# The first group of an FFN as a split group, fed in smaller jobs, with ring pieces between them

## The reference

```python
    x = x + rms_norm(y, norm_mix_post[l])          # y: the mixer's w_out product
    h = rms_norm(x, norm_ffn_pre[l])
    f = conv_gated_mlp(h, w_up[l], conv_ffn_w[l], conv_ffn_bias[l], w_down[l])
    x = x + rms_norm(f, norm_ffn_post[l])

def conv_gated_mlp(h, w_up, conv_w, conv_b, w_down):
    up = h @ w_up                                  # 2048 -> 2 * 5632
    up = causal_depthwise_conv(up, conv_w) + conv_b    # 3 taps over the tokens
    gate, val = jnp.split(up, 2, axis=-1)
    return (jax.nn.silu(gate) * val) @ w_down
```

## Time and profile before

| | us |
|---|---|
| median of 3 runs (lowest, highest) | 2581.59 (2580.73, 2586.28) |
| the profiled execution | 2575.56 |
| its span | 2573.8 |
| TensorE busy | 2519.6 (98%) |
| VectorE busy | 1678.2 (65%) |
| ScalarE busy | 1140.7 (44%) |
| weight loads and weight reads, moved | 547.89 MB, 213 GB/s |

### The profile page before, as it was taken

The page is one execution under the profiler, slowest core; times in us unless marked ns, Lnnn a source line. Parts: engine busy times, 40 slices in busy tenths (PEclk is TensorE's granted clock), DMA queues, the critical chain, the costliest instruction groups (busy, mean ns, idle before and its releaser), DMA issues.

```text
span 2573.8 us, 42624 instructions
## 1 busy us (share of the span) xinstructions
PE 2519.6 (98%) x18920; PEld 2367.0 (92%) x18920; DVE 1678.2 (65%) x2034; ACT 1140.7 (44%) x1311; POOL 11.2 (0%) x24
## 2 busy tenths in 40 slices
PE   6999999999999999999999999999899999999998
PEld 2688799999998999999999999899899889988997
DVE  5366666677787755555555579877677556764775
ACT  3422555544445434434434553054455445443554
POOL 0000000000000000000000000000000000000000
PEclk9999999999999999999999999999999999999999
DMA  9976665577885755555555555455355555555543
GB/s 399 372 245 231 217 223 199 207 293 293 304 290 201 288 194 184 193 192 186 196 184 193 182 179 188 153 184 177 151 180 197 196 194 184 195 185 192 191 172 129
DMA packets 77223, 547.89 MB, mean 213 GB/s; under 512 B 8848, under 2 KB 8976, under 8 KB 12272
## 3 DMA queue, kind: packets, MB, share of 16 engines
q1 hardware_dynamic: 74304, 533.53, 57.8%
q0 software_dynamic: 2448, 11.14, 1.2%
q10 hardware_dynamic: 288, 0.50, 0.1%
HBM read 539.90 MB, written 5.24 MB: 212 GB/s over the span
## 4 chain that ended last, share of the span: by engine, by line
PE 94%; DVE 3%; DMA 2%; ACT 1%; issue 1%; SPq 0%; DVEq 0%; ACTq 0%
PE acc L295 23%; PE acc L299 23%; PE acc L297 22%; PE acc L315 5%; PE acc L316 5%; PE acc L317 5%; PE acc L352 3%; DMA raw<-in_w_mod 1%; PE mp L382 1%; PE mp L315 1%; PE mp L317 1%; PE mp L316 1%; DVE macc L426 1%; DVE wlo L263 1%; PE mp L441 0%
## 5 line engine op out<-in xcount | busy, mean ns | idle before, releaser
L263 DVE TENSOR_TENSOR wlo<-raw,whi 128x1024 fp32r<-128x1024 f32 x779 | 942.1, 1223 | 660.2 <-ACT whi L254 658.5
L254 ACT ACTIVATE whi<-raw 128x1024 fp32r<-128x1024 f32 x779 | 817.8, 1058 | 1164.4 <-PE acc L299 860.1
L295 PE MATMUL acc<-hh,whi 128*128 128x256 f32 x3360 | 938.9, 279 | 7.7 <-issue 5.5
L299 PE MATMUL acc<-hl,whi 128*128 128x256 f32 x3360 | 941.3, 280 | 0.0
L297 PE MATMUL acc<-hh,wlo 128*128 128x256 f32 x3360 | 934.3, 278 | 0.0
L295 PEld LDWEIGHTS acc<-hh,whi 128*128 128x128 f32 x3360 | 635.6, 189 | 12.9 <-issue 11.3
L299 PEld LDWEIGHTS acc<-hl,whi 128*128 128x128 f32 x3360 | 631.9, 188 | 0.0
L297 PEld LDWEIGHTS acc<-hh,wlo 128*128 128x128 f32 x3360 | 630.1, 188 | 0.5
L299 PE MATMUL acc<-ml,whi 128*128 128x256 f32 x1536 | 430.1, 280 | 0.0
L295 PE MATMUL acc<-mh,whi 128*128 128x256 f32 x1536 | 426.6, 278 | 0.1
L297 PE MATMUL acc<-mh,wlo 128*128 128x256 f32 x1536 | 426.5, 278 | 0.0
(11 more groups left out here) (341 smaller groups left out, 2197.8 us busy)
## 6 DMA issues: line engine op xcount, KB each, us to landing
raw<-in_w_in SPq DMA_DIRECT2D x98, 1024.0 KB, 4.9
raw<-in_w_mod SPq DMA_DIRECT2D x96, 1024.0 KB, 5.8
raw<-in_w_up SPq DMA_DIRECT2D x88, 1024.0 KB, 4.9
raw<-in_w_mlp_in SPq DMA_DIRECT2D x64, 1024.0 KB, 4.9
raw<-in_w_mlp_out SPq DMA_DIRECT2D x64, 1024.0 KB, 4.9
raw<-in_w_down SPq DMA_DIRECT2D x44, 1024.0 KB, 4.9
raw<-in_w_out SPq DMA_DIRECT2D x32, 1024.0 KB, 5.1
raw<-in_w_fourier_out SPq DMA_DIRECT2D x8, 1024.0 KB, 6.1
```

The lines of the kernel that those rows point to most:

```text
L254: nc.scalar.activation(ring(whi, xh, st.p), raw_slot(k)[:, 2 * GC * j:2 * GC * (j + 1)], ACT.Copy)\
L263: nc.vector.tensor_tensor(ring(wlo, xl, st.p), raw_slot(k)[:, 2 * GC * j:2 * GC * (j + 1)], ring(whi, xh, st.p).bitcast(f32), ALU.subtract ...
L295: nc.tensor.matmul(dst, whi[:, r, cols], hi[:, kt, :], start=begin, stop=False, skip_group_check=True)
L299: last = nc.tensor.matmul(dst, whi[:, r, cols], lo[:, kt, :], start=False, stop=kt == nkt - 1, skip_group_check=True)
```

## The change

The four plain slots of the FFN's first group become four ordinary slots, so that group is split like the others, and the order of the loads becomes the ordinary one. Its x comes in nine jobs: two of one tile and seven of two. ScalarE writes `hh` directly from x with the gain; `hf` is not made. VectorE makes `hl` per tile (one instruction: x times gain minus `hh`) one job behind x, with a ring piece behind some jobs (`FFN_BEHIND`, plus one behind the third). Three more pieces stand around the two folds. `feature_piece` has a hook `tile`, which waits for each tile's job. `zz_sums` moves from before the last slot of the first group to before the fourth piece of the second. In `ffn_pair` the exceptions for the first group go. Cut to its core:

```diff
-STREAM += "d" * (MLP_CHUNKS * 32 - 16 + 12 + 2) + "ffff" * 3 + "d" * (2 + 6 + 16 + 2) + "ffff"
-STREAM += "d" * (2 + 20 * 4 + 44)
+STREAM += "d" * (MLP_CHUNKS * 32 - 16 + 12 + 2) + "ffff" * 3 + "d" * (2 + 6 + 16)
+STREAM += "d" * (2 * 4 + 20 * 4 + 44)
...
-        N2_JOBS = [(0, 1), (1, 1), (2, 2), (4, 4), (8, 4), (12, 4)]
+        N2_JOBS = [(0, 1), (1, 1)] + [(a, 2) for a in range(2, KT, 2)]
+        FFN_BEHIND = (0, 0, 0, 1, 1, 1, 1, 0, 0)
...
-                    last = nc.scalar.activation(hf[:, kt, :], xT2[:, kt, :], ACT.Copy,
+                    last = nc.scalar.activation(hh[:, kt, :], xT2[:, kt, :], ACT.Copy,
                                                 scale=pcol("norm_ffn_pre_2", kt))
-                last.then_inc(S["hf_ok"], 1)
-                act.wait_ge(S["hf_ok"], i + 1)
-                nc.scalar.activation(hh[:, a:a + n, :], hf[:, a:a + n, :], ACT.Copy).then_inc(S["fh_ok"], 1)
+                last.then_inc(S["fh_ok"], 1)
+                C(st, FFN_BEHIND[i], met=0)
+            C(st, 3, met=0)
...
+            next_x(0)
+            for i, (a, n) in enumerate(N2_JOBS):
+                if i + 1 < len(N2_JOBS):
+                    next_x(i + 1)
+                dve.wait_ge(S["xm_ok"], i + 1)
+                dve.wait_ge(S["fh_ok"], i + 1)
+                for kt in range(a, a + n):
+                    last = nc.vector.scalar_tensor_tensor(hl[:, kt, :], xT2[:, kt, :], pcol("norm_ffn_pre_2", kt),
+                                                          hh[:, kt, :].bitcast(f32), ALU.mult, ALU.subtract)
+                last.then_inc(S["fl_ok"], 1)
+                if i == 2:
+                    C(1, met=0)
+                C(FFN_BEHIND[i], met=0)
+            C(1, met=0)
             fold(xy, um1, False, "xy_ok")
+            C(1, met=0)
             dve.wait_ge(S["gy_sq"], 4)
             dve.wait_ge(S["yy_ok"], 3)
             fold(yy, um2, False, "yy_ok")
-            for i, (a, n) in enumerate(N2_JOBS):
-                dve.wait_ge(S["fh_ok"], i + 1)
-                nc.vector.tensor_tensor(hl[:, a:a + n, :], hf[:, a:a + n, :], hh[:, a:a + n, :].bitcast(f32),
-                                        ALU.subtract).then_inc(S["fl_ok"], 1)
             C(1, met=0)
             dve.wait_ge(S["zz_ps"], 1)
...
-            def zz_sums(s):
-                if s == 3:
+            def zz_sums(k0):
+                if k0 == 6:
...
-                        if c + p + v:
-                            mm_feature(pe, st, v, hh, hl, 1, ready=split if c + p == 0 else None)
+                        first = c + p == 0
+                        mm_feature(pe, st, v, hh, hl, 1, each=zz_sums if first and v else None,
+                                   tile=next_ready if first and not v else None)
```

More of the change, by code:

```diff
@@ L283, in group_done, with feature_piece @@
             eng.wait_ge(S["used"], st.e)
-        def feature_piece(pe, st, i, hi, lo, k0, nkt=KT, w=GC):
+        def feature_piece(pe, st, i, hi, lo, k0, nkt=KT, w=GC, tile=None):
             r = st.p % 4
@@ L290, in feature_piece @@
                 kt = k0 + k
+                if tile:
+                    tile(kt)
                 for t in range(w // P):
@@ L326, in acc_wait, with mm_feature @@
             st.f[i] += evictions
-        def mm_feature(pe, st, i, hi, lo, frees, nkt=KT, w=GC, ready=None, free=None, each=None):
+        def mm_feature(pe, st, i, hi, lo, frees, nkt=KT, w=GC, ready=None, free=None, each=None, tile=None):
             if free:
@@ L339, in mm_feature @@
                     each(k0)
-                feature_piece(pe, st, i, hi, lo, k0, nkt, w)
+                feature_piece(pe, st, i, hi, lo, k0, nkt, w, tile)
         def plain_group(pe, st, i, h, frees, each, between, n):
@@ L1003, in ffn_pair @@
                 for v in range(2):
[L1004 to L1010, removed]
+                    st.e += 8
+                    group_done(act, st)
+                    hi_piece(act, st)
                     act.wait_ge(acc_free[v], F_OUT2[v] + n + 2 * c + 1)
@@ L1019, in ffn_pair @@
                     last.then_inc(S["ct_ok"], 1)
-                    if n + v:
-                        hi_piece(act, st)
+                    hi_piece(act, st)
                     act.wait_ge(S["cd_ok"], 2 * n + v + 1)
@@ L1640, in _, with next_x @@
             own(nc.vector.reciprocal(rstd[:, 0, :], root[:, :]))
-            for i, (a, n) in enumerate(N2_JOBS):
+            def next_x(i):
+                a, n = N2_JOBS[i]
                 if a == 12:
@@ L1669, in ffn_pair @@
                 for v in range(2):
-                    if n < v:
-                        C(7, met=8)
-                    elif n:
-                        st.e += 8
-                    if n + v:
-                        group_done(dve, st)
-                    else:
-                        dve.wait_ge(S["f_used"], 16)
+                    st.e += 8
+                    group_done(dve, st)
                     up, um = ((up1, um1), (up2, um2))[v]
@@ L1695, in ffn_pair @@
                     last.then_inc(S["cd_ok"], 1)
-                    if n + v:
-                        lo_piece(dve, st)
+                    lo_piece(dve, st)
                     if v == 0:
@@ L1710, in ffn_pair @@
                             .then_inc(S["fid_ok"], 1)
-                    if n + v:
-                        C(4 if n + v == 11 else 6, met=0)
+                    C(4 if n + v == 11 else 6, met=0)
             def down_add(c, g):
@@ L2028, in _, with next_ready @@
                 last.then_inc(S["yq_ps"], 1)
-            def hf_each(kt):
-                for i, (a, n) in enumerate(N2_JOBS):
-                    if kt == a:
-                        pe.wait_ge(S["hf_ok"], i + 1)
-            def zz_sums(s):
-                if s == 3:
+            def next_ready(kt):
+                pe.wait_ge(S["fl_ok"], jobs_upto(kt + 1, N2_JOBS))
+            def zz_sums(k0):
+                if k0 == 6:
                     for k, total, sem in ((0, xy, "xy_ok"), (1, yy, "yy_ok")):
@@ L2042, in zz_sums @@
                     last.then_inc(S["zz_ps"], 1)
-            plain_group(pe, st, 0, hf, 1, hf_each, zz_sums, 3)
-            def split(s):
-                pe.wait_ge(S["fl_ok"], jobs_upto(4 * s + 4, N2_JOBS))
             def ffn(st, c, pairs, slots):
```

14 lines of the change are left out of this document (3 added, 11 removed).

## The result

| | before | changed |
|---|---|---|
| median, us | 2580.11 (10 runs, 2573.72 to 2586.28) | 2588.80 (10 runs, 2582.66 to 2590.94) |
| ratio, 95% interval | | 1.0036 (1.0027 to 1.0045) |
| the profiled execution, us (its span) | 2575.56 (2573.8) | 2588.48 (2586.6) |

The change makes the kernel slower by 0.36%, 9.3 us of 2580 (7.0 to 11.6). The forecast was 2588.7 and slower by 7.1 us; it stood on a median of 2581.59 from three runs of the kernel before, and ten give 2580.11. A second timing of the same kernel on another occasion gave 1.0024 (1.0015 to 1.0034). From here on "the stretch" runs from the end of the w_out_2 product (the start of the second norm's sums less TensorE's 0.69 us of idle time, 1809.39 in the trace before, 1812.50 after) to the start of the second FFN group's eviction.

A forecast was written before the change was run, and what follows sets the result against it. TensorE was taken to bound the kernel (98% busy). Terms -4.7 + 2.0 + 6.7 + 2.9 + 0.2 gave +7.1 us: 2588.7 us for the runs, 2582.7 for a profiled execution; range 2582.5 to 2595.

The forecast's parts named there:

- The plain group's 27.9 us against 22.1 and the first group's end: First FFN group: split matmuls replace slower plain fp32 ones, VectorE sets the pace, group ends 4.7 us earlier.
- VectorE's 3.5 us for a pair: First group: product and additions 1.52, two lo parts 0.84, ring piece 1.15 us, against TensorE's 2.77 us per pair.
- The sums outside the first group, 2.0 us: Third norm's sums now run within the second FFN group instead of the first, adding 2.0 us there.
- The wait behind the sums, 6.7 us: Second group: TensorE idles 6.7 us for lo piece 12, behind VectorE's third-norm factor and first eviction.
- Piece 13 behind the taps and the lower clock, 2.9 + 0.2 us: Second group: piece 13 waits behind VectorE's taps, adding 2.9 us; the clock's late return adds 0.2.
- The first rival: Clock falls in the first group's 2.4 us gap: group ends 1.8 us later, total up to +11 us; chance 0.15.
- the later one (piece 13): First rival's further price: if the clock also stays low for piece 13, 2.2 us more.
- a clock that is low through the whole group: First rival's extreme: all eight first-group pieces at 5.0 us, 12 us more than forecast.
- The second rival: Weight-slot fetch before the sums is dearer in ordinary runs, so removing it saves more: 2582.7 to 2585.6 us; chance 0.17.
- The third: Wait behind the sums is covered by a misread on-chip order: -2.7 us, 2578.9; chance 0.06.

The follow-up runs named there:

- the filler: Changed kernel plus 14 fp32 matmuls, results unread, behind the third norm's sums to keep TensorE working during its wait; stretch 71.26 us, ratio 1.0025.
- the new job sizes alone: Kernel before with only the x jobs resized to two of one tile and seven of two, plain group kept; stretch 66.68 us, ratio 1.0004.
- the kernel before with its slot released early: Kernel before with VectorE's one ring piece moved ahead of the two folds, releasing the fourth plain weight slot earlier; stretch 60.67 us, ratio 0.9986.
- the sums first: Changed kernel with the third norm's sums ahead of the second FFN group's first ring piece instead of its fourth; stretch 62.69 us, ratio 0.9994.
- nobody waiting for the sums: Changed kernel with VectorE leaving out the third norm's chain from the sums, so the FFN is scaled wrongly; stretch 60.64 us, ratio 0.9989.
- the two pieces ahead of the taps: On top of the sums first, ring pieces 12 and 13, not one piece, stand ahead of the first eviction's taps; stretch 60.48 us, ratio 0.9977.

## Why the prediction was right

- **The plain group's 27.9 us against 22.1 and the first group's end.** Forecast 4.7 us earlier, measured 4.5 (36.3 against 40.8 us into the stretch). VectorE's 3.5 us for a pair is 3.45. That VectorE sets the pace is shown by the run in which 1.67 us of it were taken out: 1.31 came back.
- **The sums outside the first group, 2.0 us.** 1857.09 to 1859.02, 1.93.
- **The wait behind the sums, 6.7 us.** 6.61. Taking away what VectorE waits for (stretch 60.6), or moving the sums ahead by three pieces (62.7), takes it away.
- **Piece 13 behind the taps and the lower clock, 2.9 + 0.2 us.** The eviction-to-eviction time was 19.60 and 19.43; with the filler, at the full clock, 19.42. So the two prices do stand in for one another, as the working had it, and the 0.2 for the clock was nothing. The clock came back 4.4 us after the restart (1865.59 to 1870.0), not 5.5 to 6; the row that the working read for the first group gives 5.3 for the kernel before (0.55 over 1816 to 1822), and its 0.80 for 1814 to 1815 gives a fall 2.5 us after TensorE stopped at 1812.07, not 2.8. The first bears on the 0.2 alone, the second on no term.
- **The first rival (the clock stays low).** It did not come in the changed kernel's two profiles, but its mechanism is real: at or just behind the 2.1 us wait within the first group the clock fell in two of the four variants that have it. Its price there was 0.8 and 1.2 us, not 1.8, and the later one (piece 13) did not come. The working's price for a clock that is low through the whole group, 12 us more, is 11.3 by its own numbers (1856.8 less 1845.5).
- **The second rival (the fetch is dearer in ordinary runs).** Removing the wait gave 2.5 us in the trace, 1.7 of them the wait itself, and 3.6 (1.5 to 5.9) in the timed runs, so not all 6 us between the profiled execution and the median can lie in the fetch. What they go with is the clock in the rest of the kernel, which the working did not look at: see the start of the stretch, below.
- **The third (the stall is covered).** Excluded by the trace.
- The forecast's median, 2588.7, met 2588.8 partly by luck: the kernel before came out 1.5 us lower than the forecast's base, and the difference larger. The two timings give 9.3 us (7.0 to 11.6) and 6.2 us (3.9 to 8.8), and 7.1 lies in both intervals, in the first only just.

One thing the working left out: when the clock rises after the first wait differs from run to run, from 3.3 to 6.1 us behind the restart in the twelve profiles. That cost the split group nothing, since VectorE was the slower one; in the kernel before it moved the 96 plain records by 0.93 us.

## What to carry to other kernels

When an engine's work is moved to where another engine needs its answer, list what stands behind the waiting instruction in that engine's order and how much work the first engine has in hand; here three ring pieces (8.3 us) covered a chain of 6.5 us when the sums stood ahead of them, and none did when they stood behind. Replacing a slower form of a matmul by a faster one gained 4.5 us and lost the cover that the slower one gave. Test a suspected price by the order first: the edit that repaired this one moved four matmuls.

## What the runs showed of the hardware

**Two paces of the same matmuls.** A 128x256 matmul of a split group starts every 115.6 ns or every 117.8 ns, at a granted clock of 1.00 in both. 1152 of them take 133.12 or 135.68 us. The last run of matmuls ahead of the second eviction begins, behind a wait or behind fp32 matmuls, at the slower pace, and in ten of the twelve profiles it passes to the faster one within 3 us, with no wait between. In the version with the new job sizes alone the first 11 steps take 118 ns each and the next 16 take 115.6:

```profile
1853.75 0.28 PE L297 MATMUL acc<-hh,wlo 128*128 128x256 f32 x1
...
1855.05 0.28 PE L295 MATMUL acc<-hh,whi 128*128 128x256 f32 x1
...
1856.90 0.28 PE L297 MATMUL acc<-hh,wlo 128*128 128x256 f32 x1
```

In the changed kernel's second profile the pace changes 2.6 us after the restart for piece 13 (20 steps from 1869.02 to 1871.38, then 22 to 1873.92). In its first profile and in the kernel before with its slot released early this change does not come, and the slower pace stays for the whole of the next six groups. In the six groups behind the second eviction it was 117.8 in the changed kernel's first profile and in the kernel before with its slot released early, 115.6 in the ten other profiles, the changed kernel's second among them. The records differ too: over 1890 to 1990 the median record of the three kinds (hi x hi, hi x lo, lo x hi) is 277, 278 and 280 ns in the kernel before, and 281, 278 and 278 ns in the changed one. What draws the one or the other, and what holds the slower one, is open; it was not tried.

**The start of a stretch moves by 6 us.** TensorE's instructions ahead of it are the same in all twelve profiles, and it started between 1809.3 and 1815.8 us. The start goes with the granted clock of the first 60 us: 0.91 in the profile of the kernel before (start 1809.39), 0.89 in three (1809.27, 1809.38, 1810.12), 0.83 to 0.86 in seven (1810.05 to 1815.51), 0.80 in the last (1815.75). Behind the second eviction all twelve take about 701.2 us, or 703.8 at the slow pace. The timed runs fit this: of the 77 executions of the kernel before that were timed beside the experiments, the six with a mean granted clock of 0.994 have a median of 2575.9 us, the 32 at 0.992 one of 2580.9, the two at 0.990 one of 2583.2. The profiled execution, 2575.56, was at 0.994. That the clock is the cause of the 6 us is a reading of these numbers; no run set it. Differences of one profile against another are only worth reading inside a stretch.

**The clock after short waits.** At the first group's wait of 2.09 to 2.13 us, which six profiles have, it fell with the sums first (at the wait's end) and with the filler (0.6 us behind it), and not in the changed kernel's two, with nobody waiting for the sums, or with the two pieces ahead of the taps. A fall came with a wait of 2.53 us (0.4 us behind it) and one of 3.41 us (within it); none came with 1.69 us. Here the Trainium skill, "TensorE: Matmul & The Clock Gate", section "HAM oscillation — how this bites in real kernels", agrees in kind: a wait for data can cost more than itself. The filler's run adds that it need not: behind the 6.61 us wait the fall cost nothing, since VectorE set the pace there.
